# State-space outputs by chunks in staggered quarters, the gated output's first column group between them, the last norm by halves, the masks loaded later

## What is computed

```python
u = (h @ w_in).reshape(bsz, seq, N_GROUPS, SSM_GROUP)          # 64 groups of 16 channels
bu = einsum('blgh,gph->blgp', u, bb)                           # complex, 64 states per group
_, _, s_re, s_im = lax.associative_scan(combine, (a, bu), axis=1)
y = (einsum('blgp,ghp->blgh', s_re, c_re) - einsum('blgp,ghp->blgh', s_im, c_im) + d_skip * u)
z = gelu(y) @ w_glu                                            # 1024 x 2048
x = x + z[..., :D_MODEL] * sigmoid(z[..., D_MODEL:])
...                                                            # all the rest of both blocks
x = layernorm(DN_ALPHA * x + 0.5 * swiglu(x, ffn_w13[1, 1], ffn_w2[1, 1]), ln_g[1, 2], ln_b[1, 2])
```

## Time and profile before

| | |
|---|---|
| median of 3 runs | 2151.14 us (2150.44 to 2151.72) |
| the profiled execution's own time | 2149.54 us |
| its span | 2147.4 us |
| TensorE busy | 2073.5 us, 97% of the span |
| VectorE busy | 1437.3 us, 67% |
| ScalarE busy | 1079.4 us, 50% |
| mean granted TensorE clock | 0.989 |
| loaded from memory | 338.14 MB, 158 GB/s over the span |

### The profile page before, as it was taken

How to read it: one execution, slowest core, us unless ns; L and a number is a source line. 1 busy time by engine, 2 the same in 40 slices (tenths; PEclk the granted TensorE clock), 3 DMA queues, 4 the chain that set the end, 5 groups by cost and what they waited for, 6 DMA issues and landing times.

```text
span 2147.4 us, 34685 instructions
## 1 busy us (share of the span) xinstructions
PE 2073.5 (97%) x15044; PEld 1798.6 (84%) x15044; DVE 1437.3 (67%) x1654; ACT 1079.4 (50%) x1276; POOL 155.7 (7%) x119
## 2 busy tenths in 40 slices
PE   7789999999999999999999999999999999999998
PEld 6778888988888888898778889888889977788886
DVE  8867775567765664775767776466558576677754
ACT  6565653565653553456544355345435564444541
POOL 1000000000001000340000020020005200002000
PEclk9699999999999999999999999999999999999999
DMA  7245555534655665564412466556546533136653
GB/s 153 51 155 162 179 188 169 193 99 156 196 187 167 204 190 188 170 210 143 132 41 99 147 206 202 189 178 197 186 157 213 190 118 118 42 118 189 197 179 122
DMA packets 259504, 342.49 MB, mean 159 GB/s; under 512 B 23352, under 2 KB 169438, under 8 KB 259352
## 3 DMA queue, kind: packets, MB, share of 16 engines
q1 hardware_dynamic: 253984, 329.95, 48.2%
q0 software_dynamic: 2768, 9.08, 1.4%
q10 hardware_dynamic: 2599, 1.23, 0.5%
HBM read 338.14 MB, written 2.10 MB: 158 GB/s over the span
## 4 chain that ended last, share of the span: by engine, by line
PE 84%; DVE 7%; ACT 4%; DMA 2%; issue 2%; POOL 0%; SPq 0%; DVEq 0%; ACTq 0%
PE acc L1987 11%; PE acc L1989 11%; PE acc L1988 11%; PE trp L2166 10%; PE acc L2166 8%; PE trp L2167 5%; PE acc L2167 4%; PE acc L2003 3%; PE trp L1987 2%; DVE w_lo L1254 2%; PE trp L1988 2%; PE trp L1989 2%; PE acc L2010 2%; DMA raw<-in_w_in 1%; PE acc L2052 1%
## 5 line engine op out<-in xcount | busy, mean ns | idle before, releaser
L1254 DVE TENSOR_TENSOR w_lo<-raw,w_hi 128x2048 fp32r<-128x2048 f32 x314 | 722.9, 2305 | 430.2 <-ACT w_hi L743 428.5
L743 ACT ACTIVATE w_hi<-raw 128x2048 fp32r<-128x2048 f32 x314 | 590.2, 1880 | 572.2 <-PE acc L1989 214.7
L2166 PE MATMUL trp<-xT,w_hi 128*128 128x512 f32 x960 | 339.7, 398 | 0.0
L2166 PE MATMUL acc<-xT,w_hi 128*128 128x512 f32 x768 | 271.6, 397 | 0.0
L2167 PE MATMUL trp<-xT,w_lo 128*128 128x256 f32 x960 | 269.4, 281 | 0.0
L2166 PEld LDWEIGHTS trp<-xT,w_hi 128*128 128x128 f32 x960 | 180.3, 188 | 44.1
L2167 PE MATMUL acc<-xT,w_lo 128*128 128x256 f32 x768 | 215.5, 281 | 0.0
L1989 PE MATMUL acc<-w_hi,hT_lo 128*128 128x512 f32 x528 | 209.3, 396 | 0.0
L1987 PE MATMUL acc<-w_hi,hT_hi 128*128 128x512 f32 x528 | 209.3, 396 | 0.0
L1988 PE MATMUL acc<-w_lo,hT_hi 128*128 128x512 f32 x528 | 209.3, 396 | 0.0
L1987 PE MATMUL acc<-xT,w_hi 128*128 128x256 f32 x704 | 199.9, 284 | 3.3 <-DVE w_lo L1254 3.1
(11 more groups left out here) (429 smaller groups left out, 3448.6 us busy)
## 6 DMA issues: line engine op xcount, KB each, us to landing
raw<-in_ffn_w SPq DMA_DIRECT2D x184, 512.0 KB
raw<-in_w_in SPq DMA_DIRECT2D x60, 1024.0 KB
raw<-in_ffn_w_up SPq DMA_DIRECT2D x88, 512.0 KB
raw<-in_ffn_w SPq DMA_DIRECT2D x40, 1024.0 KB
raw<-in_ffn_w_down SPq DMA_DIRECT2D x20, 1024.0 KB
raw<-in_ssm_w_glu SPq DMA_DIRECT2D x16, 512.0 KB
raw<-in_kv_w SPq DMA_DIRECT2D x8, 1024.0 KB
raw<-in_w_branch_a SPq DMA_DIRECT2D x8, 1024.0 KB
```

The costliest lines, as they stand in the source:

```text
L743: A(w_hi[:, p % SPL, 0:kt, :], raw[:, p % RAW, 0:kt, :], ACT.Copy).then_inc(hi_ready, 1)
L1254: V_.tensor_tensor(w_lo[:, p % SPL, 0:kt, :], raw[:, p % RAW, 0:kt, :], w_hi[:, p % SPL, 0:kt, :].bitcast(F32), ALU.subtract).then_inc(lo_ ...
L2166: mm(tile, w_hi[:, p % SPL, k, c], xT[:, k0 + k], start=i == k == 0, stop=False, skip_group_check=True)
```

## The change

- `uT` is written in the order token-in-chunk, chunk: `ssm_in` evacuates by four ScalarE instructions instead of one, which read PSUM with a step of four tokens. `token_lags` then reads contiguous runs. The matmuls of `within` read `uT` contiguously and write `y` with a step.
- `E` gets memory of its own (that of `CAm` before, where `BT` lay earlier). It no longer waits for `K_ready`. `split_lo(4)` moves ahead of it, `split_hi(4)` and `split_hi(5)` to before `within`, `split_hi(6)` to right behind it.
- `cam`, `clear` and the 256 small matmuls are gone. Instead, for each quarter g of 8 pairs: `outputs_by_chunk(g)` has 32 matmuls with a 64 x 64 piece of `E` as the stationary and 64 columns of `CA` as the moving operand, with chunks on the output's partitions; ScalarE copies the 128 x 512 result to SBUF (`by_chunks`, in the memory of `Bm`); `outputs_by_channel(g)` turns it back and adds it to `y` with 4 matmuls against the identity.
- The first column group of `glu` is cut into four pieces `gated_inputs(q)` of 12 matmuls, and these stand between the quarters. `output_rest(0)` (the `xT_lo` of quarter 0) goes between quarters 2 and 3 of `E` on VectorE, `output_rest(1)` behind quarter 3, then `split_lo(5)`, `output_rest(2)`, `split_lo(6)`, `output_rest(3)`.
- `keep_warm(n)`, n matmuls of the identity with itself, stands before `within` (8) and in three places among the quarters (2 each).
- The masks are loaded ahead of panel 18 instead of 9, and TensorE waits for them before `turn_norm("mix1")`.
- The last norm runs by tokens: `norm_out(name, 0)` stands right behind the first half's moments, ahead of the second half's residual addition, and each works and stores by halves of 512 columns.

```diff
-                if p == SPL + 6:
+                if p == gemms["up0"][0][0] + 6:
                     sp.wait_ge(sem("E_ready"), 4)
                     sp.dma_start(cst[:, P:C_PAIR], T["const_masks"][:, P:C_PAIR]).then_inc(sem("masks_in"), 16)
...
-                    A(uT[:, 4 * j:4 * j + 4, :], A4(u), ACT.Copy).then_inc(*freed(u))
+                    of = A4(u).rearrange("p f (c q j) -> p j f q c", c=8, q=8)
+                    for at in range(Q):
+                        ins = A(uT[:, 4 * j:4 * j + 4, at * NC_:at * NC_ + NC_].rearrange("p f (q c) -> p f q c", c=8), of[:, at], ACT.Copy)
...
-                        of = uT[32 * k:32 * k + 32, fs, :].rearrange("p f (c q j) -> p f q c j", c=8, q=8)[:, :, :, :, Q - 1 - lag]
+                        of = uT[32 * k:32 * k + 32, fs, (Q - 1 - lag) * NC_:(Q - lag) * NC_]
...
             for q in range(4):
-                if q < 2:
-                    cam(2 * q + 4)
-                    cam(2 * q + 5)
+                act.wait_ge(sem("chunks_filled"), 4 * (q + 1))
+                of = turn_banks[q % 2][:, :].rearrange("p (a n h) -> p a n h", a=2, h=GH)[:, :, 0:4 * Q]
+                A(by_chunks[:, q].rearrange("p (n a h) -> p a n h", a=2, h=GH), of, ACT.Copy).then_inc(sem("chunks_copied"), 1)
                 if q >= 2:
                     act.wait_ge(sem("ylo_ready"), q - 1)
-                act.wait_ge(sem("across_done"), 4 * (2 * q + 2))
+                act.wait_ge(sem("across_done"), q + 1)
                 ins = A(y_gelu[q % 2], y_tiles(2 * q, 2), ACT.Gelu_apprx_tanh)
...
-            dve.wait_ge(sem("K_ready"), 4)
-            wait_filled(dve, use["BT"] + 7)
+            split_lo(4)
             step(V_.memset(E[:, :, :, 0, 0], 0.0))
...
                 dve.sem_inc(sem("E_ready"), 1)
-
-            split_lo(4)
-            for q in range(4):
-                dve.wait_ge(sem("yhi_ready"), q + 1)
+                if g == 2:
+                    output_rest(0)
+            output_rest(1)
             split_lo(5)
+            output_rest(2)
             split_lo(6)
+            output_rest(3)
...
+            def outputs_by_chunk(g):
+                pe.wait_ge(sem("E_ready"), g + 1)
+                for k in range(4):
+                    for r in range(2):
+                        for a in range(2):
+                            for f in range(2):
+                                rows, at = slice(a * ST, a * ST + ST), f * 64 + k * GH
+                                ins = mm(o[f * NC_:f * NC_ + NC_, a, :, k, :], E[rows, r, 8 * g + 4 * f + k], CA[rows, g, :, r, at:at + GH],
+                                         start=k == r == 0, stop=r == 1, skip_group_check=True)
+            def outputs_by_channel(g):
+                pe.wait_ge(sem("chunks_copied"), g + 1)
+                for j in range(Q):
+                    ins = mm(y[:, :, :, :, j], by_chunks[:, g, j * P:j * P + P], ident, start=False, stop=j == Q - 1, skip_group_check=True)
+                ins.then_inc(sem("across_done"), 1)
...
+            keep_warm(2)
+            outputs_by_chunk(0)
+            keep_warm(2)
+            outputs_by_channel(0)
+            outputs_by_chunk(1)
+            keep_warm(2, trp[1])
+            outputs_by_channel(1)
+            outputs_by_chunk(2)
+            gated_inputs(0)
+            outputs_by_channel(2)
+            outputs_by_chunk(3)
+            gated_inputs(1)
+            outputs_by_channel(3)
+            gated_inputs(2)
+            gated_inputs(3)
+            for j in range(1, 4):
+                tokens("glu", j, use["glu"] + j, xs)
...
-            def norm_out(name):
+            def norm_out(name, t):
                 dve.wait_ge(sem("gain_in"), 32 * (naturals[name] + 1))
+                halves = (slice(0, PN), slice(PN, D))
+                for c in halves:
+                    step(V_.scalar_tensor_tensor(xn[:, t, c], x[:, t, c], mv[:, t, 0:1], gb[:, 0, c], ALU.subtract, ALU.mult))
+                dve.wait_ge(sem("root_ready"), TT * norms[name] + t + 1)
+                for n, c in enumerate(halves):
+                    step.settle(1 - n)
+                    V_.scalar_tensor_tensor(x[:, t, c], xn[:, t, c], nrm[:, 3, t:t + 1], gb[:, 1, c], ALU.mult, ALU.add).then_inc(sem("out_ready"), 1)
```

More of the change, by code:

```diff
@@ L249, in build @@
         s1b = ExitStack()
-        CAm = sb("CAm", [P, RING, Q, 2, 4, 32], F32, s1b)
+        E = sb("E", [P, 2, PAIRS, 8, 8], F32, s1b)
         s1b.close()
@@ L629, in _ @@
                     sp.dma_start(slot[:, :, half:PN], src[:, :, c1:c1 + half]).then_inc(raw_loaded[p % RAW], 16)
[L630 to L633, removed]
+            for n in range(2 * TT):
+                t, c = n // 2, slice(n % 2 * PN, n % 2 * PN + PN)
+                sp.wait_ge(sem("out_ready"), n + 1)
+                sp.dma_start(out[0, t * P:t * P + P, c], x[:, t, c]).then_inc(sem("out_stored"), 16)
+            sp.wait_ge(sem("out_stored"), 32 * TT)
         @block.gpsimd
@@ L910, in _ @@
                 driven(f)
+            split_hi(4)
+            split_hi(5)
             act.wait_ge(sem("K_ready"), 4)
@@ L924, in within @@
                     A(Kbds[h % 2][:, :, :, g * GH:g * GH + GH], lags[:, 2 * h:2 * h + 2], ACT.Copy, scale=const(C_PAIR + g, 1)).then_inc(sem("Kbd_ready"), 1)
[L926 to L944, removed]
-            clear(3)
-            within(3)
-            step.settle()
-            for f in range(RING):
-                cam(f)
-            split_hi(4)
-            split_hi(5)
+            for h in range(4):
+                within(h)
+            split_hi(6)
             act.wait_ge(sem("ftab_stored"), 16)
             for q in range(4):
-                if q < 2:
-                    cam(2 * q + 4)
-                    cam(2 * q + 5)
+                act.wait_ge(sem("chunks_filled"), 4 * (q + 1))
+                of = turn_banks[q % 2][:, :].rearrange("p (a n h) -> p a n h", a=2, h=GH)[:, :, 0:4 * Q]
+                A(by_chunks[:, q].rearrange("p (n a h) -> p a n h", a=2, h=GH), of, ACT.Copy).then_inc(sem("chunks_copied"), 1)
                 if q >= 2:
                     act.wait_ge(sem("ylo_ready"), q - 1)
-                act.wait_ge(sem("across_done"), 4 * (2 * q + 2))
+                act.wait_ge(sem("across_done"), q + 1)
                 ins = A(y_gelu[q % 2], y_tiles(2 * q, 2), ACT.Gelu_apprx_tanh)
@@ L2275, in _, with keep_warm @@
             wait_evacuated(pe, use["ssm_in1"])
+            def keep_warm(n, bank=trp[3]):
+                for _ in range(n):
+                    mm(bank[:, 0:P], ident, ident, start=True, stop=True, skip_group_check=True)
+            pe.wait_ge(sem("bu_copied"), 8)
+            keep_warm(8)
             for f in range(8):
@@ L2285, in _ @@
                 ins.then_inc(sem("within_done"), 1)
-            for f in range(8):
-                y = y_tiles(f)[:, 0].rearrange("p (c q j) -> p q c j", q=8, j=Q)
-                pe.wait_ge(sem("CAm_ready"), 2 * (f + 1))
-                pe.wait_ge(sem("E_ready"), f // 2 + 1)
-                for j in range(Q):
-                    for r in range(2):
-                        for k in range(4):
-                            rows = slice(32 * k, 32 * k + 32)
-                            ins = mm(y[rows, :, :, j], CAm[:, f % RING, j, r, k, :], E[:, r, 4 * f + k], start=False, stop=r == 1, skip_group_check=True)
-                            if j == Q - 1 and r == 1:
-                                ins.then_inc(sem("across_done"), 1)
```

65 lines of the change are left out of this document (40 added, 25 removed).

## The result

The changed kernel takes 2136.51 us, the median of 4 runs (2134.79 to 2142.33), against 2151.18 for the kernel before beside it; the ratio is 0.9937 (0.9917 to 0.9956). On a second chip it was 2138.78 (2135.50 to 2140.12, 5 runs) against 2149.98, ratio 0.9943 (0.9930 to 0.9955). The forecast was 2139.3, 0.55% faster, and came true in sign and size: 14.7 us were gained on the first chip and 11.2 on the second, against 11.8 forecast. The profiled execution of after is the slowest of its four (2142.33), so I read it beside the profile of the second chip (2137.97), called `after_again`.

What follows compares the result with a forecast made beforehand. Bounds: VectorE's chain up to E's first quarter, then ScalarE, and TensorE from the second column group. Gains 7.8 + 2.15 + 1.8 = 11.8 us from 2149.54 give 2137.8; the median 1.6 above gives 2139.3, range 2133.5 to 2145.

Steps and rivals of the forecast that it cites:

- The inputs: ScalarE's lag copies and ssm_in evacuation: copies give back 4.4 us, evacuation takes 2.1 against 1.03, net about 3.3.
- The states: E on VectorE: starts at 90.8 instead of 93.86, first quarter ready at 107.1 instead of 110.18.
- within: Product on TensorE ahead of the quarters: ends between about 98 and 105, covered by E by 2 us or more.
- The quarters: TensorE from E's first quarter: 20.4 work, 0.8 waits, 1.8 half clock; first column group done at 130.1, 7.8 us gained.
- The gap: TensorE's wait for panel 11's split in the second column group goes: 2.15 us gained.
- The masks at panel 18: Masks loaded ahead of panel 18 fit there: zero cost, with 2.15 us as the upper bound.
- The tail: Last norm and stores at the kernel's end: gain between 1.0 and 2.6 us, 1.8 taken.
- the lag copies got faster: Answers the rival that token_lags copies get no faster: 1.6 us worse, 2140.9; chance 0.17.
- The clock did not stay up: Answers the rival that TensorE's clock stays up through the wait for E: 1.8 us better, 2137.5; chance 0.13.
- No panel was late: Answers the rival of a late panel, in the gap's place or at panel 18: 2.15 us worse, 2141.5; chance 0.09.
- The stepped PSUM write: Rival: outputs_by_channel's stepped write to y takes twice its time per record, 3.9 us more, 2143.2; chance 0.05.
- The slower rival: TensorE's clock falls waiting for E and doesn't rise in the quarters: up to 18.6 us more, 2158; chance 0.03.

Runs made afterwards that it cites:

- undo_layout: Changed kernel with uT's token order as before: one evacuation instruction, lag copies that read with a step; 2140.34 us.
- no_keep_warm: Changed kernel without any of its keep_warm (8 ahead of within, three times 2 among the quarters); 2136.74 us, one execution.
- lo4_late: Changed kernel with split_lo(4) between E's second and third quarters and split_hi(6) ahead of the third gelu; 2137.19 us.
- lo4_third: Changed kernel with split_lo(4) behind E's third quarter and split_hi(6) ahead of the fourth gelu; 2138.62 us, one execution.

## Why the prediction was right, point by point

- **The inputs**: right by two errors. The lag copies take 413 ns, not 378, so 16 give back 3.8 instead of 4.4; the stepped evacuation from PSUM takes 1.21, below both of my bounds (1.5 to 2.6), since the four instructions overlap and the step costs hardly anything there (385 ns each, against 378 for a contiguous one). Net 3.7 against the 3.3 forecast. The 2.8 us of `bu` waits went, and `undo_layout` brings them back with the copies' old form.
- **The states**: `E` starts at 90.91 (90.8 forecast), its first quarter is ready at 107.24 (107.1), the fourth at 116.96 (116.5).
- **`within`** ended at 100.7 and 101.6 in the two traces of the changed kernel, ahead of the first quarter, as forecast (98 to 105). In the other runs it ended at 96.4 to 102.4, and at 106.7 in `undo_layout`.
- **The quarters**: 23.6 us from 107.24 to 130.84, where the sum had 23.0. The mis-sized term is the clock. It came back at 113.0 (111.9 in `after_again`), not 3 to 4 us after 107.1, and half rate cost 2.6 rather than 1.8: 0.8 in the first `outputs_by_chunk` (1.99 against 1.16), 0.5 in `keep_warm`, 0.9 in the first `outputs_by_channel`, 0.3 in the next `outputs_by_chunk`. The waits of 0.8 were 0.16: `keep_warm` covers the copy. I had booked `keep_warm` as 1.0 of cost; in `no_keep_warm` the mark is 2.3 to 2.9 later without it.
- **The gap** went, for 2.4 with what lies around it, as forecast at 2.15. But the step named both the masks and the splits, and gave the masks' old place a price of 2.15 as an upper bound; in the changed kernel that price is zero, and each alone would have been enough.
- **The masks at panel 18** cost nothing: TensorE has no wait there.
- **The tail**: 3.0 from the last addition on and 2.8 with the push, above my bounds (1.0 to 2.6). Behind the last addition four instructions of 512 take 2.7 instead of 4.98 (2.3), and the last store's half of the bytes another 0.7 (2140.5 - 2138.07 = 2.4 against 3.2), which I had named and not added up. The root doesn't hold the second step: it takes 0.99 (at 2135.50 in after), not 1.52, beside instructions of 512. The addition is pushed back by 0.2, the lower end of what I had given.
- **The rivals**: the lag copies got faster. The clock did not stay up, in any of these traces. No panel was late where I looked; one was late where I didn't, 700 us on, for 2.2 on average. The stepped PSUM write costs nothing that these rows show: 8 records of `outputs_by_channel`, whose neighbours are 32 elements apart, take 1.05, as 8 contiguous ones of the same shape at 167.54 take 1.09. `within`, whose write has the same step now and had runs of one to four elements before, took 2.57 to 2.59 for 16 records at full clock against 2.70, and 2.60 to 2.67 with the old order in `undo_layout`. The Trainium skill's sentence (SBUF — State Buffer, section Door 1: The DMA port swizzle) isn't borne out here. The slower rival had a real mechanism, which `no_keep_warm` shows for 11.5 us; with `keep_warm` it lasted 4.6 to 5.6.

- **Two slips**: the earlier trace rows has three slices below nine tenths at the start, not four. The range's low end is 0.6 lower than its own terms give (2139.3 less 1.8, 0.8, 1.6 and 1 is 2134.1, not 2133.5); the measured 2136.51 is inside either way.

The sum was 11.8. In the profiled execution stage, gap and tail came to 12.5, and 5.5 of it was lost between the mixer and the end, which no step of the prediction had; near 900 us such a loss is 2.2 on average. The medians gained 14.7 and 11.2. So the mechanisms were right step by step, but that the total came so close is in part luck: the tail was undersized, the half clock too, and the loss was missing. Why the first chip gained 3.5 more than the second isn't known, since no trace of its faster executions was kept.

## What to carry to other kernels

Where TensorE alternates between short bursts and waits on another engine, cost every piece at half clock unless something fills the waits, and fill the waits between the bursts before the long one ahead of them. A gap at the end of a chain of buffers is short of slack by its own length only: look for any step of the chain that can be moved, and don't credit the gain to one. Judge parts worth 2 to 3 us by marks in the trace, and read on behind the edited stage, since the order in which two engines collide, and the time that a load takes, can change hundreds of us later where nothing was edited.

## What the runs showed of the hardware

- The granted clock fell in every trace of the changed form in the wait between `within` and the quarters or just behind it: from 2.3 (`no_keep_warm`) to 4.9 us (after) after TensorE's last work, and in `lo4_late` and `lo4_third` when the quarters had already begun, after waits of only 2.73 and 2.53. It also fell near 65 us in after, while L2224 ran behind a wait of only 1.20, and those 64 records took 11.48. In five of the ten traces with such a wait (1.18 to 1.20) it fell there, and L2224 took 11.48 to 12.42; in the other five it stayed, and L2224 took 7.33, with `within` ending at 96.4 to 97.4 (99.6 in `no_keep_warm`) instead of 100.7 to 102.4.
- ScalarE reads SBUF with neighbours 128 bytes apart at 654 ns for 32 x 256 and contiguously at 413; from PSUM with the same step, an instruction of 128 x 256 took 385 ns and four of them 1.21 us together, and one contiguous of 1024 took 1.03.
- VectorE's split of 128 x 2048 takes 2.29 us alone and 4.47 to 4.56 when it starts just behind a GpSimd instruction that reads SBUF; two GpSimd multiplications go from 4.79 to 6.85 when the split comes first.
